# First block: head sums by column groups, roots by a square root of ScalarE and one Newton step

## The reference, cut to what matters

```python
h = rms_norm(x, attn_norm_g[l])                  # sqrt of the mean square over 1024 channels
z = h @ w_in[l]
a_val, a_gate, p_in, q, k, v = jnp.split(z, splits, axis=-1)
...
q = rms_norm(q.reshape(b_, s_, DIFF_HEADS, 2, DIFF_HEAD_DIM), q_norm_g[l])
k = rms_norm(k.reshape(b_, s_, DIFF_HEADS, 2, DIFF_HEAD_DIM), k_norm_g[l])
...
lam = (exp(sum(lambda_q1 * lambda_k1)) - exp(sum(lambda_q2 * lambda_k2)) + lam_init)
o = diff_attention(q, k, v, lam, slopes)
```

## Time and profile before

| | us |
|---|---|
| median of 3 runs | 1721.42 |
| lowest, highest | 1720.37, 1721.43 |
| profiled execution, its time | 1721.62 |
| its span | 1719.5 |

### The profile page before, as it was taken

One profiled execution on the slowest core, in us unless ns is written; L12 is line 12 of the kernel. 1 busy time (PEld: TensorE's weight loads), 2 busy tenths in 40 slices (PEclk: granted clock), 3 DMA queues, 4 the chain that ended last, 5 costly groups with the idle time before them and its releaser, 6 DMA issues.

```text
span 1719.5 us, 36871 instructions
## 1 busy us (share of the span) xinstructions
PE 1705.7 (99%) x13876; PEld 1646.5 (96%) x13876; DVE 1175.9 (68%) x2048; ACT 857.2 (50%) x1399; POOL 282.9 (16%) x317
## 2 busy tenths in 40 slices
PE   8999999999999999999999999999999999999998
PEld 8999999999999999888999999999999888999998
DVE  7587756767665567676886655766567666787754
ACT  5465544544444355545554444444437554654443
POOL 1030000011000111632420002000112455330001
PEclk9999999999999999999999999999999999999999
DMA  7445555555555554333555555555545343555554
GB/s 272 145 136 182 184 182 186 183 184 182 173 171 171 175 169 148 124 128 109 170 184 171 171 176 172 179 171 172 177 154 178 129 160 106 165 191 186 185 184 135
DMA packets 84902, 288.72 MB, mean 168 GB/s; under 512 B 9152, under 2 KB 16192, under 8 KB 84544
## 3 DMA queue, kind: packets, MB, share of 16 engines
q1 hardware_dynamic: 80448, 283.08, 49.8%
q10 hardware_dynamic: 4352, 4.20, 0.8%
HBM read 285.89 MB, written 1.34 MB: 167 GB/s over the span
## 4 chain that ended last, share of the span: by engine, by line
PE 96%; DVE 2%; ACT 1%; issue 1%; DMA 0%; POOL 0%; SPq 0%; DVEq 0%; ACTq 0%
PE PS L950 29%; PE PS L952 29%; PE PS L951 29%; PE PS L1431 1%; PE PS L1465 1%; PE PS L1439 1%; PE PS L1469 1%; PE PS L1449 1%; DVE w_lo L1616 1%; PE PS L1150 0%; PE PS L1410 0%; ACT w_hi L502 0%; DMA h<-xT 0%; PE PS L1455 0%; PE PS L1405 0%
## 5 line engine op out<-in xcount | busy, mean ns | idle before, releaser
L950 PE MATMUL PS<-x_hi,w_hi 128*128 128x272 f32 (+1 forms) x2832 | 818.7, 289 | 4.5 <-DVE x_lo L1621 1.7
L1616 DVE TENSOR_TENSOR w_lo<-raw,w_hi 128x1024 fp32r<-128x1024 f32 x522 | 655.2, 1259 | 237.1 <-ACT w_hi L502 227.7
L952 PE MATMUL PS<-x_hi,w_lo 128*128 128x272 f32 (+1 forms) x2832 | 810.1, 286 | 0.0
L951 PE MATMUL PS<-x_lo,w_hi 128*128 128x272 f32 (+1 forms) x2832 | 808.1, 285 | 0.0
L502 ACT ACTIVATE w_hi<-raw 128x1024 fp32r<-128x1024 f32 x522 | 548.0, 1056 | 466.8 <-PE PS L952 463.3
L950 PEld LDWEIGHTS PS<-x_hi,w_hi 128*128 128x128 f32 x2832 | 535.3, 189 | 13.7 <-issue 8.5
L952 PEld LDWEIGHTS PS<-x_hi,w_lo 128*128 128x128 f32 x2832 | 535.6, 189 | 0.0
L951 PEld LDWEIGHTS PS<-x_lo,w_hi 128*128 128x128 f32 x2832 | 534.8, 189 | 0.3
L950 PE MATMUL PS<-a_hi,w_hi 128*128 128x272 f32 (+1 forms) x1280 | 364.8, 285 | 1.3 <-DVE a_lo L2279 1.3
L952 PE MATMUL PS<-a_hi,w_lo 128*128 128x272 f32 (+1 forms) x1280 | 363.7, 284 | 0.0
L951 PE MATMUL PS<-a_lo,w_hi 128*128 128x272 f32 (+1 forms) x1280 | 363.0, 284 | 0.0
(11 more groups left out here) (321 smaller groups left out, 1273.5 us busy)
## 6 DMA issues: line engine op xcount, KB each, us to landing
raw<-stream SPq DMA_DIRECT2D x522, 512.0 KB, 3.3
biasB<-rpbz ACTq DMA_DIRECT2D x16, 256.0 KB, 3.2
G<-b1mats SPq DMA_DIRECT2D x2, 1024.0 KB, 7.1
raw<-stream SPq DMA_DIRECT2D x6, 256.0 KB, 5.8
h<-xT SPq DMA_DIRECT2D x4, 272.0 KB, 4.6
mat<-mats SPq DMA_DIRECT2D x1, 952.0 KB, 5.2
out<-qk SPq DMA_DIRECT2D x3, 256.0 KB, 2.4
v_tok<-u_rows SPq DMA_DIRECT2D x4, 142.0 KB, 3.1
```

The lines of the kernel that those rows point to most:

```text
L950: pe.matmul(ps, hi, rh, start=first, stop=False)
L951: pe.matmul(ps, hi, rl, start=False, stop=False)
L952: return pe.matmul(ps, lo, rh, start=False, stop=last)
L1616: dve.tensor_tensor(w_lo[:, slot, :], raw[:, slot, :], w_hi[:, slot, :].bitcast(F32), ALU.subtract).then_inc(lo_done, 1)
```

## The change

- `head_sums` keeps tokens along the free axis: for each of the four tiles one matmul with 32 selector columns as weights and the 256 squares as moving data, each into its own group of 32 output partitions.
- `head_spread` follows: row 32t + m of the roots (256 tokens) is spread over 64 partitions, with a column of the identity as weights.
- `first_stat` has only the form with tokens along the free axis; the epsilon of the heads becomes a row, `eps_row`, computed from it on VectorE.
- The roots of x and of the heads: ScalarE takes a square root, VectorE a reciprocal and one Newton step (`sqrt_root`). They are 272 and 256 columns wide, in the buffer `PT`. Each needs a handover to ScalarE and back, at steps 3, 5 and 15 of ScalarE's order, ahead of the split of that step. The convolution's roots stay as they are.
- The first activation of the kernel is a Sqrt instead of a Copy, and a one-element Sqrt stands at the end of step 14, ahead of that step's split.

```diff
@@ -239,8 +239,8 @@
         pool_w = late[:, 1648:1904].rearrange("p (i c) -> p i c", i=2)
         head_sq = S_f[:, 0:4 * SEQ].rearrange("p (j t) -> p j t", j=4)
         o_tok = [S_f[:, 1536 + SEQ * i:1536 + SEQ * (i + 1)] for i in range(2)]
-        eps_ms, lam_sum, lam_e, lam = small[:, 96:98], small[:, 98:100], small[:, 100:102], small[:, 102:103]
-        head_ms, head_rs = small[:, 104:120], small[:, 120:136]
+        lam_sum, lam_e, lam = small[:, 98:100], small[:, 100:102], small[:, 102:103]
+        head_ms, head_rs, head_t0, head_t1, eps_row = (PT[:, i * SEQ:(i + 1) * SEQ] for i in range(5))
         root0, root1 = small[:, 136:152], small[:, 152:168]
         o_ssq, o_rs = small[:, 168:176], small[:, 176:184]
         conv_ms, conv_rs = small[:, 184:186], small[:, 186:188]
@@ -292,6 +292,8 @@
         in_free = [sem(f"in_free{i}") for i in range(2)]
         misc_out, misc_free = sem("misc_out"), [sem(f"misc_free{i}") for i in range(2)]
         qk_raw, head_root, qk_scaled = sem("qk_raw"), sem("head_root"), sem("qk_scaled")
+        first_ms, first_sqrt, head_meaned, head_sqrt = (
+            sem("first_ms"), sem("first_sqrt"), sem("head_meaned"), sem("head_sqrt"))
         scores1_out, turned1_done, probs1_copied, pv1_out = (
             sem("scores1_out"), sem("turned1_done"), sem("probs1_copied"), sem("pv1_out"))
         probs1_mixed, o_squared, o_scaled, o_turned = sem("probs1_mixed"), sem("o_squared"), sem("o_scaled"), sem("o_turned")
@@ -569,7 +571,7 @@
                 act.activation(in_squares[:, m, :], h[:, m, :], ACT.Square).then_inc(x_squared, 1)
 
             act.wait_ge(warm_ready, 1)
-            act.activation(S_f[:, 384:385], S_f[:, 0:1], ACT.Copy)
+            act.activation(S_f[:, 384:385], S_f[:, 0:1], ACT.Sqrt)
             act.wait_ge(cols_landed, 16)
             x_split_hi(0)
             half_split_hi(0, 0)
@@ -582,6 +584,11 @@
                 half_split_hi(n, 0)
                 half_split_hi(n, 1)
 
+            def head_root_of(j):
+
+                act.wait_ge(head_meaned, j + 1)
+                act.activation(head_rs, head_ms, ACT.Sqrt).then_inc(head_sqrt, 1)
+
             def head_tile(c):
 
                 kind, i = IN1_ORDER[c]
@@ -685,6 +692,13 @@
                     for m in range(KD // 2 + 1, KD):
                         square_in(m)
                     split_hi(AHEAD, AHEAD)
+                if c == 3:
+                    act.wait_ge(first_ms, 1)
+                    act.activation(rstd[:, :], ms, ACT.Sqrt).then_inc(first_sqrt, 1)
+                if c == 5:
+                    head_root_of(0)
+                if c == 15:
+                    head_root_of(1)
                 if c == 6:
                     act.wait_ge(lam_exp, 1)
                     act.activation(lam_e, lam_sum, ACT.Exp).then_inc(lam_exp, 1)
@@ -712,6 +726,7 @@
                     head_mix_hi(0)
                     head_mix_hi(1)
                     conv_square()
+                    act.activation(small[:, 96:97], zero, ACT.Sqrt)
                 if c == 16:
                     conv_silu()
                 if c == 17:
@@ -1049,12 +1064,7 @@
                 pe.wait_ge(squares_summed, 1)
                 pe.matmul(PS[:, b, 0:L], ones, acc, start=True, stop=False, skip_group_check=True)
                 pe.wait_ge(half_summed, 1)
-                pe.matmul(PS[:, b, 0:L], ones, half_acc, start=False, stop=True, skip_group_check=True)
-                for u in range(2):
-                    to = PS[:, b, L + 2 * u:L + 2 * u + 2]
-                    pe.matmul(to, acc[:, u * P:(u + 1) * P], ones[:, 0:2], start=True, stop=False, skip_group_check=True)
-                    mm = pe.matmul(to, half_acc[:, u * P:(u + 1) * P], ones[:, 0:2], start=False, stop=True, skip_group_check=True)
-                mm.then_inc(misc_out, 1)
+                pe.matmul(PS[:, b, 0:L], ones, half_acc, start=False, stop=True, skip_group_check=True).then_inc(misc_out, 1)
 
             def head_sums(j):
 
@@ -1064,13 +1074,11 @@
                         c = IN1_AT[kind, i]
                         pe.wait_ge(in_free[c % 2], in_bank_uses(c))
                 for t in range(4):
-                    for u in range(2):
-                        at = 8 * u + 2 * t
-                        mm = pe.matmul(PS[:, b, at:at + 2], head_sq[:, t, u * P:(u + 1) * P], mat[:, M_SEL16:M_SEL16 + 2],
-                                       start=True, stop=True, skip_group_check=True)
+                    mm = pe.matmul(PS[32 * t:32 * t + 32, b, 0:SEQ], mat[:, M_SEL16:M_SEL16 + 32], head_sq[:, t, :],
+                                   start=True, stop=True, skip_group_check=True)
                 if j == 0:
                     pe.wait_ge(lam_products, 1)
-                    mm = pe.matmul(PS[:, b, 32:34], ones[0:64, :], small[0:64, 38:40], start=True, stop=True, skip_group_check=True)
+                    mm = pe.matmul(PS[:, b, SEQ:SEQ + 2], ones[0:64, :], small[0:64, 38:40], start=True, stop=True, skip_group_check=True)
                 mm.then_inc(misc_out, 1)
 
             def head_spread(hd):
@@ -1078,12 +1086,10 @@
                 b = misc(f"spread{hd}")
                 pe.wait_ge(head_root, hd // 2 + 1)
                 for x in range(2):
-                    for u in range(2):
-                        for m in range(2):
-                            at = 8 * u + 4 * (hd % 2) + 2 * x + m
-                            mm = pe.matmul(PS[64 * m:64 * m + 64, b, x * SEQ + u * P:x * SEQ + (u + 1) * P],
-                                           head_rs[:, at:at + 1].to_broadcast([P, 64]), ident, start=True, stop=True,
-                                           skip_group_check=True)
+                    r = 32 * (2 * (hd % 2) + x)
+                    for m in range(2):
+                        mm = pe.matmul(PS[64 * m:64 * m + 64, b, x * SEQ:(x + 1) * SEQ], ident[:, r + m:r + m + 1].to_broadcast([P, 64]),
+                                       head_rs, start=True, stop=True, skip_group_check=True)
                 mm.then_inc(misc_out, 1)
 
             def values_turn(j):
@@ -1772,13 +1778,21 @@
 
                 ins.then_inc(misc_free[misc_bank(e) % 2], 1)
 
+            def sqrt_root(x, y, t0, t1, rooted, k, done):
+
+                dve.wait_ge(rooted, k)
+                step(dve.reciprocal(y, y))
+                step(dve.tensor_tensor(t0, y, y, ALU.mult))
+                step(dve.scalar_tensor_tensor(t1, t0, -0.5, x, ALU.mult, ALU.mult))
+                dve.scalar_tensor_tensor(y, t1, 1.5, y, ALU.add, ALU.mult).then_inc(done, 1)
+
             def first_mean_square():
 
                 b = misc("stat")
-                step(dve.tensor_scalar(ms, PS[:, b, 0:L], 1.0 / D, EPS, ALU.mult, ALU.add))
-                misc_read("stat", dve.tensor_scalar(eps_ms.unsqueeze(2), PS[:, b, L:L + 4].rearrange("p (u x) -> p u x", u=2)[:, :, 0:1],
-                                                    EPS / D, EPS * EPS, ALU.mult, ALU.add))
-                inverse_root(ms, rstd[:, :], rstd_done, 1, G[:, 21, :], G[:, 23, :])
+                dve.tensor_scalar(ms, PS[:, b, 0:L], 1.0 / D, EPS, ALU.mult, ALU.add).then_inc(first_ms, 1)
+                dve.wait_ge(first_ms, 1)
+                misc_read("stat", dve.tensor_scalar(eps_row, ms[:, 0:SEQ], EPS, None, ALU.mult))
+                sqrt_root(ms, rstd[:, :], G[:, 21, :], G[:, 23, :], first_sqrt, 1, rstd_done)
                 dve.wait_ge(rstd_done, 1)
 
             def in_tile(c, to):
@@ -1792,16 +1806,12 @@
                 b = misc(e)
                 if j == 0:
                     dve.wait_ge(misc_free[misc_bank("stat") % 2], misc_uses("stat"))
-                    dve.tensor_copy(lam_sum, PS[:, b, 32:34]).then_inc(lam_exp, 1)
-                for u in range(2):
-                    ins = dve.tensor_scalar(head_ms[:, 8 * u:8 * u + 8], PS[:, b, 8 * u:8 * u + 8], 1.0 / HD, eps_ms[:, u:u + 1],
-                                            ALU.mult, ALU.add)
-                    if u == 0:
-                        step(ins)
-                    else:
-                        misc_read(e, ins)
-                dve.wait_ge(misc_free[misc_bank(e) % 2], misc_uses(e))
-                inverse_root(head_ms, head_rs, head_root, 1, root0, root1)
+                    dve.tensor_copy(lam_sum, PS[:, b, SEQ:SEQ + 2]).then_inc(lam_exp, 1)
+                    dve.wait_ge(lam_exp, 1)
+                dve.scalar_tensor_tensor(head_ms, PS[:, b, 0:SEQ], 1.0 / HD, eps_row, ALU.mult, ALU.add).then_inc(head_meaned, 1)
+                dve.wait_ge(head_meaned, j + 1)
+                misc_read(e, dve.tensor_copy(small[0:1, 93:94], small[0:1, 94:95]))
+                sqrt_root(head_ms, head_rs, head_t0, head_t1, head_sqrt, j + 1, head_root)
 
             def head_scale(hd):
 
```

## The result

The changed kernel takes 1724.51 us, median of 18 runs (1723.47 to 1726.13), against 1721.34 us for the kernel before, median of 18 runs (1719.69 to 1721.80). The ratio is 1.002 with a 95% interval of 1.0013 to 1.0027: 3.2 us slower. Its profiled execution took 1723.47 us, the lowest of the 18, with a span of 1721.7.

The account below looks back on a forecast made before the run. TensorE, busy 99% of the span, was taken as the bound. Its lead and delay, -0.85 + 2.17 = +1.3 us, plus 3.0 us for the clock made +4.3 us: 1725.5 us, range 1721.8 to 1727.2.

Parts of the forecast that it names:

- only one spell: Rival: one half-clock spell instead of two follows TensorE's stands, +2.8 us, 1724.2 us; chance 0.29.
- the first place: Statistic of x, sums and spreads of heads 0 and 1, 20 to 35 us: 2.0 us stand, TensorE 0.85 us ahead.
- the second place: Sums and spreads of heads 2 and 3, from 73 us: stands of 1.8 and 3.4 us, TensorE 2.17 us later.
- no change: Bound for telling a difference: about 0.2%, 3.44 us, line at 1724.9 us; chance of same 0.46.
- TensorE's work: Statistic 0.81 us, head sums 2.69 us and spreads 0.26 us less: 3.8 us less to do.
- The sums: Head sums as four column-group matmuls: 0.44 us per call, 1.34 us less for each of two calls.
- The spreads: Head spreads with 256 moving columns: 0.88 us per head against 0.95, 0.26 us less in all.
- VectorE's prices: Wide root steps: reciprocal 1.83 us for 272 columns and 1.73 us for 256, other steps about 0.47 us.
- a drain of about 1380 ns: Rival: the table switch for heads 2 and 3 also drains ScalarE, +1.4 us, 1726.9 us; chance 0.06.
- The clock: One half-clock spell after the stand at 30.3 us and one after those from 77.9 us: 2 x 1.5 = 3.0 us.
- the old spell at 77 us: Half clock over chunk 15 in the kernel before, 1.5 us, expected to go with the small matmuls.
- slower: Outcome above the 1724.9 us line: chance 0.48, from most of the forecast (0.43) and the drain case (0.06).

Follow-up runs that it names:

- the filled kernel: The changed kernel with idle matmuls put into TensorE's two stands, three ahead of the convolution's spread and seven ahead of head 2's: 1722.76 us, ratio 1.0009.
- the run with the narrow root: The kernel before with only the heads' roots by ScalarE square root, reciprocal and Newton step, 16 columns wide on the old layout: 1720.78 us, ratio 0.9999.

## Why the prediction was right, and where it was off

- **Range and sign.** 1724.51 us lies within 1721.8 to 1727.2, 1.0 us under the 1725.5 forecast. Of the cases it is the rival "only one spell" (1724.2): in the profiled execution the stand of 2.08 us at the first place brought no half clock, the one of 3.27 us did. By the marks the second place was forecast at 2.17 + 1.5 = 3.7 us and is 3.71; the first was forecast at 1.5 - 0.85 = +0.65 us and is -0.28. Two errors met there: the spell that didn't come (1.5 us too much) and a lead that is 0.6 us smaller than worked out. That they partly cancel is luck. At +0.18% the median sits just inside the bound that I set for "no change", with an interval on both sides of it.
- **TensorE's work.** 3.8 us less was forecast, 3.5 us less is on the page; 0.45 us of these lie ahead of the statistic, where only the kernel before has a spell, and by the pieces it is 3.2. The statistic came as said: from its first matmul to the head sums it takes 25.43 - 18.75 = 6.68 us instead of 27.52 - 20.06 = 7.46, 0.78 less. The sums take 0.57 us where 0.44 was taken, so 1.2 us goes from each call and not 1.34. (the earlier trace rows themselves give 3.3 us over 63 steps, 0.052 us and not 0.055, so 0.42 for eight.) The spreads were mis-sized: 1.87 us for two heads (31.51 to 33.38) and 1.01 for one, where 0.88 was taken and 0.95 and 1.02 stood before. Wider moving data didn't help them, and the old row was the better guide than the convolution's.
- **VectorE's prices.** Reciprocal 1.85 and 1.75 us for a forecast of 1.83 and 1.73; handovers and steps as said. This was the largest step between the saving in work and the loss: the run without the reciprocal comes out level with the kernel before. The Trainium skill ("VectorE: DVE Perf Modes", First, the fixed hardware budget) has the divide repeated 8 times, which would be 2.1 us by the estimate made; the trace has 1.75, so the measurement decides for less.
- **First place.** A stand of 2.0 us was forecast, 2.08 came, and that match is partly luck. The forecast ended chunk 5 after 2.87 us, while the earlier trace rows have 33.07 - 0.35 - 29.61 = 3.11 us from its start to the wait, and the changed kernel 31.51 - 2.08 - 26.31 = 3.12; counted in that way the forecast's stand was 1.8. And the spread was to start 0.72 us earlier and, counted from the statistic's first matmul, starts only 0.25 earlier: 31.51 - 18.75 = 12.76 us against 33.07 - 20.06 = 13.01. The forecast had VectorE take the statistic 1.10 us after its first matmul; it took it 20.29 - 18.75 = 1.54 after, since it was still in a split until 20.36. The sum moved that step by the whole 0.81 us, as if the 1.0 us that VectorE idles before it were cover; the split was in the way. By how much differs between executions: the filled kernel, whose code at the first place is the same, takes the statistic 20.91 - 19.79 = 1.12 us after its first matmul, and its first stand is 1.69 us. The spreads, which didn't shrink, are the other part of the missing gain.
- **Second place.** Stands of 1.8 and 3.4 us were forecast, 1.42 and 3.27 came; the spread of head 2 was to be 2.3 us later, and from the first mark it is (82.05 - 72.12) - (81.28 - 73.71) = 2.36. Moving the Sqrt shows that 1.4 us of it is the table load. The Trainium skill ("ScalarE: Activation LUTs", What ACT_TABLE_LOAD costs) adds a drain of about 1380 ns; here the activation before it ends at 70.94 + 0.73 = 71.67, the load begins at 71.69 and lasts 1.28 us, and the next activation starts at 72.98, so no drain is seen and that rival falls.
- **The clock.** One spell of 1.4 us instead of two of 1.5. The mechanism held at the second place (filling the stand removes the spell); what was off is the count, and that the old spell at 77 us was taken as certain. The run with the old second place had none there. The small matmuls ahead of it take 76.31 - 73.71 = 2.6 us, where the prediction has 2.7.
- **What stays open.** Which stands bring a spell differs between executions: 2.08 us did not in the changed kernel's profile, 3.06 us did in the run with the old root of x, and the same second place brought 1.4 us of loss in one kernel and about 2.6 in another. The 18 times of the changed kernel lie in two groups, five at 1723.5 us (mean granted clock 0.999, the profiled one among them) and twelve from 1724.4 to 1724.8 (0.997 or 0.998), with one at 1726.1; those of the kernel before lie likewise, seven from 1719.7 to 1720.8 and eleven from 1721.3 to 1721.8. The distance fits one spell more or less, such as that at 12 us, but only one execution of each was traced.
- **The chances.** The parts were added a hundredth off: 0.43 and 0.06 make 0.49 for slower, where 0.48 stands.

## What to carry to other kernels

When a layout makes one engine's work cheaper, price the same data on every engine that touches it: going from 16 to 256 columns saved 1.2 us of matmuls per call and cost VectorE a reciprocal of 1.75 us instead of 0.25. A chain that a full engine waits for belongs behind work that this engine has anyway; the same change with a few lines of its order moved is 3.8 us faster than before instead of 3.2 slower. A function-table load belongs behind the last item of its queue that another engine is waiting for.

## What the runs showed of the hardware

- TensorE's clock fell to half with no stand at all, as at 77 us in the kernel before. In the run with the narrow root TensorE is busy without a gap from 26 to 34 us; from 26.11 to 28.19 it does 2-column matmuls, and the clock is 0.77 from 29 to 30 us and 0.50 in the two microseconds from there:
```profile
30.00:32.00 2.00, 2.00 (x12) 2.00 (x11) 1.68 (x4) 1.97 (x3) 0.00 (x0) 0.50 0.66 225
```
  The same 2.1 us of small matmuls brought no fall in the kernel before's profile. The 2.6 us of them at the second place were followed by a fall at 77 us there, and by none in the kernel with the old second place.
- A reciprocal costs by the column and not by the partition: 1834 ns for 10 partitions by 272, 1.85 us for 128 by 272, 1.75 us for 128 by 256, 0.25 us for 128 by 16.
- Four f32 matmuls of 32 weight columns in four column groups take 0.57 us up to the next instruction for 256 moving columns, 0.13 us more than the convolution's row gave. A head's spread takes 1.01 us as two pairs of 256 columns and 1.02 us as four pairs of 128.
